# Attention of a diffusion trunk on one core: scores issued two units ahead, a PSUM bank per head for the turned probabilities, per-unit division by the row sums, and RMS norms without GpSimd

## The reference, cut to what matters

```
def trunk_layer(x, mod, ...):
    h = rmsnorm(x, g_mix_pre) * (1 + scale1) + shift1
    y, ctx_state = mixer(h)                      # in-projection, attention (+ pooling), out-projection
    x = x + gate1 * rmsnorm(y, g_mix_post)
    h = rmsnorm(x, g_ffn_pre) * (1 + scale2) + shift2
    x = x + gate2 * rmsnorm(conv_ffn(h, ...), g_ffn_post)
```

## Time and profile before

| | |
|---|---|
| time, median of 3 runs | 1976.22 us (1975.79 to 1978.95) |
| profiled execution | 1974.18 us, its span 1972.2 us |
| PE busy | 1686.9 us, 86% of the span |
| DVE busy | 1133.2 us, 57% |
| ACT busy | 731.8 us, 37% |
| POOL busy | 252.8 us, 13% |
| mean granted clock of TensorE | 0.945 of full speed |

### The profile page before, as it was taken

How to read it: one execution, slowest core, us unless ns; L and a number is a source line. 1 busy time by engine, 2 the same in 40 slices (tenths; PEclk the granted TensorE clock), 3 DMA queues, 4 the chain that set the end, 5 groups by cost and what they waited for, 6 DMA issues and landing times.

```text
span 1972.2 us, 32385 instructions
## 1 busy us (share of the span) xinstructions
PE 1686.9 (86%) x11768; PEld 1547.0 (78%) x11768; DVE 1133.2 (57%) x1921; ACT 731.8 (37%) x1189; POOL 252.8 (13%) x199
## 2 busy tenths in 40 slices
PE   5697588793999999999769968776959999999994
PEld 1595466682999999999659965656849999999994
DVE  4585545566777767777763235553276662366524
ACT  3621355223544214442141136552346652244320
POOL 1451210004100000000150031310050000000003
PEclk9898799996999999999889989989979999999997
DMA  8251000150333443345322110000202222222211
GB/s 299 77 158 54 6 2 1 54 187 16 94 105 127 171 164 106 104 129 184 115 75 75 54 56 2 21 21 22 64 0 75 74 87 74 64 74 74 87 52 54
DMA packets 42797, 160.65 MB, mean 81 GB/s; under 512 B 5088, under 2 KB 6112, under 8 KB 42336
## 3 DMA queue, kind: packets, MB, share of 16 engines
q1 hardware_dynamic: 39888, 152.00, 23.5%
q0 software_dynamic: 1616, 6.68, 1.0%
q10 hardware_dynamic: 1216, 0.92, 0.2%
HBM read 156.04 MB, written 3.54 MB: 81 GB/s over the span
## 4 chain that ended last, share of the span: by engine, by line
PE 42%; DVE 5%; issue 2%; ACT 1%; POOL 0%; DVEq 0%; ACTq 0%; POOLq 0%
PE ps L1375 14%; PE ps L1376 14%; PE ps L1517 2%; PE ps L1547 2%; PE ps L1414 2%; DVE x L868 2%; PE ps L1532 1%; PE ps L1472 1%; PE ps L1473 1%; DVE work L847 1%; PE ps L1401 1%; PE ps L1427 1%; PE ps L1428 1%; PE ps L1587 1%; PE ps L1533 0%
## 5 line engine op out<-in xcount | busy, mean ns | idle before, releaser
L493 ACT ACTIVATE whi<-raw 128x1024 fp32r<-128x1024 f32 (+1 forms) x166 | 185.6, 1120 | 602.5 <-PE ps L1376 518.9
L1375 PE MATMUL ps<-hh,whi 128*128 128x320 f32 x920 | 288.6, 314 | 8.4 <-DVE wlo L777 8.4
L1376 PE MATMUL ps<-hl,whi 128*128 128x320 f32 x920 | 285.0, 310 | 0.0
L1376 PE MATMUL ps<-hh,whi 128*128 128x320 f32 x920 | 285.0, 310 | 0.0
L1375 PE MATMUL ps<-hh,wlo 128*128 128x320 f32 x920 | 285.0, 310 | 0.0
L1375 PE MATMUL ps<-hl,whi 128*128 128x320 f32 x920 | 284.9, 310 | 0.0
L1376 PE MATMUL ps<-hh,wlo 128*128 128x320 f32 x920 | 284.9, 310 | 0.0
L777 DVE TENSOR_TENSOR wlo<-raw,whi 128x1024 fp32r<-128x1024 f32 (+1 forms) x166 | 219.6, 1325 | 73.3 <-ACT whi L493 72.9
L1227 POOL TENSOR_TENSOR work<-y,work 128x640 f32<-128x640 f32 x32 | 59.7, 1870 | 1253.2 <-DVE work L847 1242.6
L1375 PEld LDWEIGHTS ps<-hh,whi 128*128 128x128 f32 x920 | 173.5, 189 | 10.6 <-DVE wlo L777 9.5
L1376 PEld LDWEIGHTS ps<-hh,whi 128*128 128x128 f32 x920 | 173.4, 189 | 1.1 <-issue 0.2
(11 more groups left out here) (211 smaller groups left out, 3599.2 us busy)
## 6 DMA issues: line engine op xcount, KB each, us to landing
raw<-in_w SPq DMA_DIRECT2D x134, 512.0 KB, 3.6
work<-in_wmodt SPq DMA_DIRECT2D x54, 512.0 KB, 3.6
raw<-in_w SPq DMA_DIRECT2D x32, 704.0 KB, 4.1
ring<-in_wmodt SPq DMA_DIRECT2D x26, 512.0 KB, 3.7
work<-in_wmod SPq DMA_DIRECT2D x16, 512.0 KB, 5.0
work<-in_rpb POOLq DMA_DIRECT2D x8, 480.0 KB, 4.4
x<-in_x SPq DMA_DIRECT2D x1, 2560.0 KB, 17.8
out_x<-x SPq DMA_DIRECT2D x8, 320.0 KB, 2.2
```

Source lines behind the costliest of these rows:

```text
L493: nc.scalar.activation(whi[:, s, 0:kk * P], raw[:, s, 0:kk * P], ACT.Copy).then_inc(s_hi, 1)
L1375: T.matmul(bankA[s], slot(w, s, k), h[:, k, 0:HT], start=st, stop=sp_)
L1376: last = T.matmul(bankB[s], slot(w, s, k), h[:, k, HT:NT], start=st, stop=sp_)
```

## The change

Five edits, all in attention and the norms:

1. PE's order in attention becomes turn a, turn b, scores of unit i+2, values of unit i; the first two units' scores are issued at the start. DVE's order becomes: copy of both turned context parts of unit i in one instruction, inverse of its sums, `neg_max` of unit i+2, take unit i. ACT's order stays.
2. Head b's turned probabilities go to bank 7; head a's stay in bank 4. The values of every unit go to bank 6 alone.
3. Each unit inverts its own two columns of sums on DVE (kind C first adds the sink's exponential), PE multiplies the two inverses with the identity beside the values in bank 6, and DVE copies the values to `y` and multiplies them there.
4. The inversion at the end, the spreads between the chunks of the out-projection and their multiplications by DVE are gone; `mix_in_hi` and `mix_in_lo` just go through the 8 chunks.
5. The scaling by the reciprocal moves from POOL to DVE's own program, one chunk of `tn` two steps ahead of its use.

```diff
@@ PE
             def turn_probs(job):
-                if j:
-                    pe.wait_ge(s_ptb, j)
+                if job.unit:
+                    pe.wait_ge(s_ptb, job.unit)
                 if not job.prompt:
-                    if job.latent:
-                        pe.wait_ge(s_pta, job.latent)
+                    if job.latent >= 2:
+                        pe.wait_ge(s_pta, job.latent - 1)
                     for c in range(job.lo, NS, P):
-                        T.transpose(ps[:, 4, c:c + P], pb[j % 4][:, c:c + P], ident[:, :])
-                T.transpose(ps[:, 5, 0:P], pb[j % 4][:, NS:NT], ident[:, :]).then_inc(s_pt, 1)
+                        T.transpose(turned_probs[half][:, c:c + P], pb[j % 4][:, c:c + P], ident[:, :])
+                T.transpose(ps[:, 5, half * P:(half + 1) * P], pb[j % 4][:, NS:NT], ident[:, :]).then_inc(s_pt, 1)
             def sum_values(unit, v):
-                if a.unit >= 2:
-                    pe.wait_ge(s_oe, a.unit - 1)
+                if a.unit:
+                    pe.wait_ge(s_oe, a.unit)
...
+                pe.wait_ge(s_rinv, a.unit + 1)
+                for job in unit:
+                    inverse = sums[:, job.unit, job.half:job.half + 1].to_broadcast([P, DH])
+                    last = T.matmul(values_bank[job.rows, P:2 * P], inverse, ident[:, :], start=True, stop=True)
                 last.then_inc(s_o, 1)
             def attention(layer, v):
-                scores(units[0])
+                for unit in units[0:2]:
+                    scores(unit)
                 for i, (a, b) in enumerate(units):
                     turn_probs(a)
-                    if i + 1 < len(units):
-                        scores(units[i + 1])
                     turn_probs(b)
+                    if i + 2 < len(units):
+                        scores(units[i + 2])
                     sum_values((a, b), v)
@@ mix_pair
-                spread(first)
-                spread(first + 1)
                 for k in range(KD):
                     pe.wait_ge(s_otl, KD * layer + k + 1)
                     pair_chunk(k)
-                    if first + 2 <= k + 2 < KD:
-                        spread(k + 2)
@@ DVE, attention
+            def copy_turned(unit):
+                dve.wait_ge(s_pt, b.index + 1)
+                if a.unit:
+                    dve.wait_ge(s_o, a.unit)
+                V.tensor_copy(pts[:, :, NS:NT], ps[:, 5, 0:2 * NP].rearrange("p (h n) -> p h n", h=2)).then_inc(s_ptb, 1)
+            def invert(unit):
+                own = sums[:, a.unit, :]
+                dve.wait_ge(s_p, a.index + 2)
+                if a.kind == "C":
+                    V.tensor_tensor(own, own, sinks[:, a.unit - 30, :], ALU.add).then_inc(s_den, 1)
+                    dve.wait_ge(s_den, a.unit - 30 + 1)
+                V.reciprocal(own, own).then_inc(s_rinv, 1)
             def take_values(unit):
                 dve.wait_ge(s_o, a.unit + 1)
-                V.tensor_copy(y[:, a.chunk, a.q0:a.q0 + P], ps[:, 6 + a.unit % 2, 0:P]).then_inc(s_oe, 1)
+                V.tensor_copy(out, values_bank[:, 0:P]).then_inc(s_ot, 1)
+                dve.wait_ge(s_ot, a.unit + 1)
+                V.tensor_tensor(out, out, values_bank[:, P:2 * P], ALU.mult).then_inc(s_oe, 1)
+                for i, unit in enumerate(units):
+                    copy_turned(unit)
+                    invert(unit)
+                    if i + 2 < len(units):
+                        for job in units[i + 2]:
+                            neg_max(job)
+                    take_values(unit)
@@ DVE, norms (the POOL function scale_rows and its eight calls are taken out)
+            def scale_row(n, src, k, s):
+                dve.wait_ge(s_rec, n + 1)
+                dve.wait_ge(s_tu, k + (8 * n + 1))
+                V.tensor_tensor(tn[s], chunk(src, k), rec, ALU.mult).then_inc(s_t, 1)
+            def rows_then(n, src, use):
+                for s in range(2):
+                    scale_row(n, src, s, s)
+                with dve.Fori(0, KD // 2 - 1) as h:
+                    for s in range(2):
+                        use(2 * h + s, s)
+                        scale_row(n, src, 2 * h + (s + 2), s)
+                for s in range(2):
+                    use(KD - 2 + s, s)
```

More of the change, by code:

```diff
@@ L852, in pre_norm, with low @@
                 reciprocal(n)
[L853 to L857, removed]
+                def low(k, s):
+                    dve.wait_ge(s_hh, k + (hidx + 1))
+                    V.tensor_tensor(chunk(hl, k), hf[s], chunk(hh, k).bitcast(F32), ALU.subtract).then_inc(s_hl, 1)
+                rows_then(n, x, low)
             def post_norm(layer, which):
@@ L862, in post_norm, with add @@
                 reciprocal(n)
[L863 to L871, removed]
+                def add(k, s):
+                    dve.wait_ge(s_t, k + (8 * n + 1))
+                    for st, f, t in SEG:
+                        xs = part(x, k, f, t - f)
+                        last = V.scalar_tensor_tensor(
+                            out=xs, in0=tn[s][:, f:t], scalar=coef[:, layer, st, which, bass.ds(k, 1)],
+                            in1=xs, op0=ALU.mult, op1=ALU.add)
+                    last.then_inc(s_tu, 1)
+                rows_then(n, y, add)
             dve.wait_ge(s_cst, 1)
@@ L1038, in attention @@
[L1038 to L1043, removed]
+                units = UNITS_OF[layer]
+                for unit in units[0:2]:
+                    for job in unit:
+                        neg_max(job)
@@ L1061, in low @@
                     V.tensor_tensor(hl[:, c, :], y[:, c, :], hh[:, c, :].bitcast(F32), ALU.subtract).then_inc(s_otl, 1)
-                first = 2 - 2 * layer
-                dve.wait_ge(s_oe, (30, 70)[layer])
-                for c in range(first):
+                for c in range(KD):
                     low(c)
[L1067 to L1074, removed]
             mix_in_lo(0)
@@ L1219, in _ @@
             G = nc.gpsimd
[L1221 to L1227, removed]
             def rope_sin(pairs, r0):
@@ L1546, in sum_values @@
                     for job in unit:
-                        last = T.matmul(bank[job.rows, 0:P], v[:, t, job.v_col:job.v_col + DH], pts[:, job.half, c:c + P],
-                                        start=i == 0, stop=i == len(keys) - 1)
+                        T.matmul(values_bank[job.rows, 0:P], v[:, t, job.v_col:job.v_col + DH],
+                                 pts[:, job.half, c:c + P], start=i == 0, stop=i == len(keys) - 1)
+                pe.wait_ge(s_rinv, a.unit + 1)
+                for job in unit:
+                    inverse = sums[:, job.unit, job.half:job.half + 1].to_broadcast([P, DH])
+                    last = T.matmul(values_bank[job.rows, P:2 * P], inverse, ident[:, :], start=True, stop=True)
                 last.then_inc(s_o, 1)
@@ L1574, in mix_pair @@
                 pe.wait_ge(s_fb, u0 + 2)
[L1575 to L1582, removed]
-                    for unit in UNITS_OF[layer]:
-                        for job in unit:
-                            if job.chunk == c:
-                                inverse = sums[:, job.unit, job.half:job.half + 1].to_broadcast([P, DH])
-                                last = T.matmul(psf[job.rows, at + job.q0:at + job.q0 + P], inverse, ident[:, :],
-                                                start=True, stop=True)
-                    last.then_inc(s_spread, 1)
-                spread(first)
-                spread(first + 1)
                 for k in range(KD):
```

46 lines of the change are left out of this document (11 added, 35 removed).

## The result

1863.62 us median of 4 runs (1860.28 to 1868.57) against 1976.01 beside it: a ratio of 0.9434, interval 0.9407 to 0.9461. The forecast was 1870 in a range of 1845 to 1905. The profiled execution has a span of 1862.3 us, 109.9 less than before.

The account below looks back on a forecast made before the run. Attention was taken as paced by waits on a chain, the norms by GpSimd's queue. Gains of 16.5 + 23.4 + 17.7 + 22.4 + 24.7 = 104.7 us from a span of 1972.2 gave 1870 on the median's terms, range 1845 to 1905.

Parts of the forecast that it names:

- The wait of 0.73: Attention: TensorE's idle before each value product, said to be covered by the new order with 0.4 us to spare.
- 17.27 + 5 x 0.28: Attention: five kind B units' busy time plus 0.28 us a unit for the inverses, 18.7 us instead of 21.67.
- my lower bound of 0.22: Attention: least cost in us on TensorE of a unit's two products with the inverses; range to 0.45, taken as 0.28.
- 4 us of it: Layer 1 attention: recovery of time lost to kind D's clock of 0.93, put at 4 of 1.5 for each of four groups.
- The last rival: Attention: TensorE's clock falls to 1.2 GHz; 2066 us if all latent units run at that level; chance 0.03.
- The rule of the Trainium skill that I set beside it: Attention: products cycling through PSUM banks with small idles swing between clock levels, so the new order's clock would fall.
- forecast 16.3: First out-projection pair: ends 16.3 us after attention, from a first product at +1.8 and eight chunks of 1.85.
- +18.0: Layer 0 modulation behind attention: next chunk 18.0 us after attention's end instead of 35.7, so 17.7 less.
- 17.9: Post norms: total gain in us for four, about 4.7 each, from a chunk of 1.80 instead of 2.33.
- where I charged 0.12: Post norms: allowance in us for a wait in each VectorE chunk, part of the 1.80 a chunk.
- the overlap of 0.08: Post norms: us taken off each chunk's 128-element addition (0.34 less 0.08) for overlap with the next instruction.
- I take 1.7 for each: Pre norms: gain of 1.7 us each from an earlier first chunk with scaling on VectorE, 6.8 for four.

Follow-up runs that it names:

- the kernels without division: Changed kernel without the two products with the inverses per unit and VectorE's multiplication (outputs then not the reference's): 1851.51 us, 0.9381 of before.
- unread products: Changed kernel plus products nobody reads, 32 (first norm 16) before and 9 behind each pre norm's first pair, 10 before each out-projection pair: 1853.39 us.
- the bank alone: Changed kernel with scores and row minima one unit ahead instead of two, keeping two turned banks: 1928.75 us, 0.976 of before.
- the lookahead alone: Changed kernel with both heads' turned probabilities in one bank, turn b again behind the scores of unit i+2: 1930.14 us, 0.9769 of before.

## Why the prediction was right, and where it was not

**Attention: right mechanism, wrong size.** The wait of 0.73 went, the copies lie under the scores, ScalarE's exponentials come in time: five kind B units take 17.50, not 18.7. The mis-sized term is "17.27 + 5 x 0.28". It added the inverses to TensorE's busy time, as if a group's busy time did not depend on what stands next to it. Turn b directly behind turn a saves 0.09 a unit (0.61 for 0.70); turn b gives way to the scores 0.63 after its start, where it took 0.77 up to the wait (252.66 - 0.73 - 251.16); and the inverses cost 0.19 to 0.21 net, below my lower bound of 0.22. Together that is nothing, as the busy times of 17.27 and 17.25 say. It makes 1.2 us for five units, 7 of layer 0's 8.4; in layer 1 five units of kind C take 13.92 and of kind D 18.35, the latter at a clock of 1.00, so all of the clock's loss there came back and not 4 us of it. The 0.97 and 0.96 of the whole stages come from their first units; behind these the level did not fall again in either layer:

```profile
228.90:331.70 102.80, 99.26 (x1160) 81.21 (x1158) 66.45 (x230) 68.21 (x162) 10.16 (x16) 1.00 0.01 2
1126.60:1252.30 125.70, 118.44 (x1390) 96.07 (x1390) 95.43 (x387) 88.37 (x249) 37.01 (x40) 1.00 0.05 18
```

The last rival did not come about: with more work and shorter gaps the clock rose (0.91 to 0.96 in layer 1). The rule of the Trainium skill that I set beside it (TensorE: Matmul & The Clock Gate, "A second HAM failure mode: psum-queue depth-cycling"), which was seen in another kernel, is not borne out by this trace: five groups a unit by turns over eight banks, with the weight load idle for 0.17 to 0.24 ahead of three of them, ran at 1.00.

**Out-projection: as worked out.** The pair's output was taken 17.0 after attention's end (forecast 16.3; eight chunks of 1.85 are 14.8, not the 14.5 in my sum, so it should have said 16.6), the first modulation chunk came at +19.3 (331.74 to 351.00), not +18.0. Two parts of it: TensorE started 1.84 after attention, as forecast, but ran at the lower level for some 14 products (clock 0.90 in the stage), and VectorE waited 0.65 for ScalarE's split of the weights where it had waited for the DMA. In layer 1 the pair ran at 0.80. Its rows at full clock had come right behind the spreads; in the run with the division after attention, where the spreads are back, both pairs ran at 1.00.

**Post norms: right.** 17.2 for 17.9. A chunk takes 1.91, not 1.80; the wait behind the addition is 0.16, where I charged 0.12, and with it goes the overlap of 0.08 that I had taken off the last addition. The Trainium skill (VectorE: DVE Perf Modes, "The DRAIN you can't avoid") would have it cost nothing, for a chain of copies; in this chain, in which the waiting instruction overwrites what the one before has read, the trace shows the 0.16 in each chunk.

**Pre norms: wrong.** The step "I take 1.7 for each" was right as far as it went: in all four the first product came 1.5 to 1.7 earlier. It failed in what came next: I had priced the supply and not the engine that receives it. In norm 6 the first product came 4.32 after the reciprocal instead of 5.87, 1.55 earlier, and yet the next reciprocal stood where it had: TensorE, woken earlier, ran 17 products of the first pair and 20 behind it at the lower level, where it had been 12 and 13. At 0.12 us each (0.267 against 0.147 from start to start) that is 1.4 of the 1.55. The first product before (the reciprocal ended at 1458.43) and after (at 1352.85):

```profile
1464.30 0.60 PE L1472 MATMUL ps<-hh,whi 128*128 128x320 f32 x1 [10.86 <-DVE hl L856]
1357.17 0.60 PE L1469 MATMUL ps<-hh,whi 128*128 128x320 f32 x1 [9.31 <-DVE hl L872]
```

Norm 2 lost its gain in the same way (28 such products for 16). In norm 4 the number was the same in both kernels (21 and 22), and there 1.5 arrived (164.2 to 162.7). In norm 0 the 1.76 lasted through the in-projection's 480 products and went only at the 32 products of the head sums behind them, some seven of which ran at the lower level. That stretch before, then after:

```profile
152.00:160.40 8.40, 8.40 (x32) 3.00 (x32) 1.72 (x4) 1.23 (x1) 0.00 (x0) 1.00 0.40 127
153.40:163.43 10.03, 10.03 (x31) 3.36 (x32) 1.73 (x4) 1.25 (x1) 0.00 (x0) 0.83 0.33 106
```

Counted over the projections behind pre norms and behind attention, there are some 130 products at the lower level and 15 us lost by them in the changed kernel, both times that it ran, against some 90 and 10.5 before. Two runs show the other outcome without any unread product: in the kernels without division and with the division after attention TensorE stayed at the higher level behind norm 6's first pair. The window of the former that answers to the 0.66 above (26.15 behind the reciprocal's start):

```profile
1359.03:1369.03 10.00, 8.55 (x58) 8.56 (x59) 7.89 (x11) 6.93 (x10) 0.00 (x0) 1.00 0.34 108
```

There the stage took 488.9 and 488.8, not 491.9. Over the runs with the norms on VectorE and without unread products, this stage follows the number of its products at the lower level: 36 to 39 with 491.9 to 492.2, 26 with 490.3, 13 to 15 with 488.8 and 488.9. So the gain of the supply arrives when the clock lets it. With unread products in every such place, the four pre norms' stages were 5.1 shorter than in the changed kernel beside it, those behind attention 3.9. Why the engine falls to the lower level behind the pair in most runs and not in all stays open.

## What to carry to other kernels

A chain of copies is hidden only when both the work to hide it and a bank for the second result are there: either alone, with the division inside, left attention no shorter in all than it had been (315 us with the bank alone and 322 with the lookahead alone, against 311). Price an added product by what it does to its neighbours' gaps, not by adding its duration to the busy time, and look whether it is one instruction or two. And whatever wakes TensorE earlier, or removes work from it in front of a dense stretch, may hand the gain to the clock; some 170 unread products around such stretches gave 9 us by their stages here, 10 by the medians.

## What the runs showed that was not expected

A 128x128 float32 product by a diagonal takes two instructions, and twice the time of a turn of the same block (1.22 against 0.61 for five blocks). The wait ahead of the inverses, which the prediction allowed up to 0.2 for, shows no idle at all when its semaphore is up (values at 285.84, inverses at 286.99). Up to the first norm's reciprocal the time differs between runs, for the same instructions, by 4.7 us (63.0 to 67.7), and one stage of dense products by 3 with the clock, which is more than some of the terms argued about here; only a comparison by stages tells them apart.
